# First eight projection tiles on raw activations, with the token's norm factor applied when they are copied out of PSUM

## What is computed

```
def rmsnorm(x, g):
    y = x * rsqrt(mean(x * x, axis=-1, keepdims=True) + EPS)
    return y * g

mk, mv = split(rmsnorm(mem, norm_mem) @ w_mem_kv)      # 256 memory rows
h = rmsnorm(x, norm_mix)
mq, mk, mv, mo, mi, mf, fq, fk, fv, ff, cq, gates = split_cols(h @ w_in)
qk_c, conv_new = causal_conv(conv_prev, concat([mq, mk]), conv_w, conv_b)
...                       # mLSTM, forgetting attention, cross-attention, gates, w_out
x = x + peer_ffn(rmsnorm(x, norm_ffn), ...)            # 16384 single-neuron experts
```

## Time and profile before

| | us |
|---|---|
| median of 3 runs | 2104.72 |
| lowest, highest | 2104.01, 2104.93 |
| the profiled execution | 2106.87 |
| its span in the trace | 2105.1 |
| PE busy (95% of the span) | 2004.1 |
| DVE busy (68%) | 1441.5 |
| ACT busy (39%) | 827.5 |
| POOL busy (38%) | 803.8 |

### The profile page before, as it was taken

The page is one execution under the profiler, slowest core; times in us unless marked ns, Lnnn a source line. Parts: engine busy times, 40 slices in busy tenths (PEclk is TensorE's granted clock), DMA queues, the critical chain, the costliest instruction groups (busy, mean ns, idle before and its releaser), DMA issues.

```text
span 2105.1 us, 34329 instructions
## 1 busy us (share of the span) xinstructions
PE 2004.1 (95%) x12622; PEld 1225.8 (58%) x12632; DVE 1441.5 (68%) x2699; ACT 827.5 (39%) x1223; POOL 803.8 (38%) x502
## 2 busy tenths in 40 slices
PE   5998998999999799999999999999899999999996
PEld 3745666667777577555555555555455555555553
DVE  5663554433335567889979999983687777777774
ACT  5334333434443322333445656663333333333331
POOL 5442111112233222466576666666343222222210
PEclk9999989999999899999999999999999999999998
DMA  5532112122344212357598999999999888889961
GB/s 200 133 129 93 41 50 79 69 73 79 139 135 132 92 61 73 134 184 243 206 336 306 351 356 359 353 358 390 354 377 369 335 331 330 330 333 342 338 236 45
DMA packets 180320, 467.11 MB, mean 222 GB/s; under 512 B 18600, under 2 KB 85168, under 8 KB 179448
## 3 DMA queue, kind: packets, MB, share of 16 engines
q1 hardware_dynamic: 102160, 248.28, 33.2%
q0 software_dynamic: 36864, 134.23, 17.4%
q10 hardware_dynamic: 41192, 83.22, 10.6%
HBM read 393.54 MB, written 72.14 MB: 221 GB/s over the span
## 4 chain that ended last, share of the span: by engine, by line
PE 81%; DVE 12%; DMA 3%; ACT 2%; issue 1%; POOL 1%; ACTq 0%; DVEq 0%
PE ps L1476 30%; PE ps L1836 27%; PE ps L1546 10%; PE ps L1492 3%; DMA rows<-in_u_rows,rowi 2%; PE ps L1693 2%; DVE rows L1322 1%; PE ps L1789 1%; PE ps L1790 1%; PE ps L1855 1%; PE ps L1658 1%; PE ps L1673 1%; PE ps L1752 1%; DVE eq L1309 1%; DMA raw<-in_v_units 1%
## 5 line engine op out<-in xcount | busy, mean ns | idle before, releaser
L479 POOL TENSOR_TENSOR w_lo<-raw,w_hi 128x1024 bf16<-128x1024 f32 x229 | 509.9, 2228 | 792.3 <-ACT w_hi L550 791.5
L550 ACT ACTIVATE w_hi<-raw 128x1024 bf16<-128x1024 f32 x357 | 375.2, 1052 | 505.3 <-PE ps L1836 299.2
L1476 PE MATMUL ps<-act_hi,w_hi 128*128 128x448 bf16 (+1 forms) x1424 | 445.6, 336 | 17.6 <-DVE act_lo L937 16.7
L1476 PE MATMUL ps<-act_lo,w_hi 128*128 128x448 bf16 (+1 forms) x1424 | 445.1, 336 | 0.0
L1476 PE MATMUL ps<-act_hi,w_lo 128*128 128x448 bf16 (+1 forms) x1424 | 445.0, 336 | 0.0
L1836 PE MATMUL ps<-W_hi,w_hi 128*128 128x448 bf16 x992 | 350.5, 353 | 7.0 <-DVE W_lo L1424 7.0
L1836 PE MATMUL ps<-W_hi,w_lo 128*128 128x448 bf16 x992 | 350.3, 353 | 0.0
L1836 PE MATMUL ps<-W_lo,w_hi 128*128 128x448 bf16 x992 | 350.3, 353 | 0.0
L492 POOL DMA_INDIRECT rows<-in_v_units,rowi x128 | 154.4, 1206 | 411.4 <-DVE accS L1419 394.9
L1405 DVE TENSOR_TENSOR w_lo<-raw,w_hi 128x1024 bf16<-128x1024 f32 x128 | 156.5, 1223 | 116.4 <-ACT w_hi L550 116.3
L1476 PEld LDWEIGHTS ps<-act_hi,w_hi 128*128 128x128 bf16 x1424 | 137.9, 98 | 123.0 <-issue 19.9
(11 more groups left out here) (333 smaller groups left out, 2937.5 us busy)
## 6 DMA issues: line engine op xcount, KB each, us to landing
raw<-in_u_units SPq DMA_DIRECT2D x128, 512.0 KB, 4.4
raw<-in_v_units SPq DMA_DIRECT2D x128, 512.0 KB, 9.3
raw<-in_units SPq DMA_DIRECT2D x101, 512.0 KB, 3.2
hd<-hb ACTq DMA_DIRECT2D x128, 224.0 KB, 5.2
gd<-gsb ACTq DMA_DIRECT2D x64, 448.0 KB, 6.4
Gb<-gd SPq DMA_DIRECT2D x32, 896.0 KB, 6.4
Hb<-hd SPq DMA_DIRECT2D x32, 896.0 KB, 8.2
gz<-stage ACTq DMA_DIRECT2D x24, 288.0 KB, 2.1
```

The source lines that it names most:

```text
L479: pool.tensor_tensor(w_lo[:, k % RING, :], raw[:, k % RAW, :], w_hi[:, k % RING, :], ALU.subtract).then_inc(lo_ready, 1)
L550: act.activation(w_hi[:, k % RING, :], raw[:, k % RAW, :], ACT.Copy).then_inc(hi_ready, 1)
L1476: last = pe.matmul(ps[:, bank + half, 0:n], w[:, slot, col:col + P], x(k)[:, half * n:(half + 1) * n], start=(k == 0 and w is w_hi and x i ...
```

## The change

- PE's eight tiles take `raw_hi` and `raw_lo`, the halves of `x * g` without the token's factor. ACT makes `raw_hi` by a copy with a scale, DVE `raw_lo` by one operation on `xT`, `par` and `raw_hi`.
- The factor is multiplied in where DVE copies a tile out: `copy_tile` is now a product of PSUM and `wk[:, 1, :]`. The tiles use three pairs of banks in turn (0 to 5), and tile k waits for the copy of tile k - 3.
- The factor is made for the token on the partition: five matmuls of one column (`spots`) sum the squares, ACT takes the root and DVE the reciprocal of 128 x 5 numbers (`rx`), and five matmuls with the identity spread them over banks 6 and 7, from where ACT copies 128 x 576 to `wk[:, 1, :]`. On PE the first five stand behind tile 0, the second five behind tile 1.
- `act_hi` and `act_lo`, with the factor, are still made, for what comes behind the eight tiles; DVE does so after it has copied out tiles 0 and 1, with tile 2's copy in the middle.
- `par` and weight unit 0 are loaded at once from SP, the table of the root is loaded while ACT waits for `xT`, and ACT casts units 0 to 3 between the eight blocks.
- PE's sums for the memory rows stand ahead of tile 6, in bank 6; ahead of tile 4 before.

```diff
@@ SP, ACT @@
+            sp.dma_start(par[:, :], a["par"]).then_inc(par_in, 16)
+            load(a["units"][0], 0, True, 0)
             sp.wait_ge(x_in[0], 16)
-            for n in range(RAW):
+            for n in range(1, RAW):
                 load(a["units"][n], n, True, 0)
...
-            act.dma_start(par[:, :], a["par"]).then_inc(par_in, 16)
...
             act.wait_ge(consts, 8)
-            square(xT, mix_sq, lambda k: (x_in[k // (KT // 2)], 16))
+            act.activation(warm[:, 3:4], epsb[:, 0:1], ACT.Sqrt)
             act.wait_ge(par_in, 16)
-            for n in range(RAW):
-                high_unit(n)
+            for k in range(KT):
+                act.wait_ge(x_in[k // (KT // 2)], 16)
+                act.activation(raw_hi[:, k, :], xT[:, k, :], ACT.Copy, scale=par[:, C_MIX + k:C_MIX + k + 1]).then_inc(x_hi, 1)
+                if k in (0, 3, 5, 7):
+                    high_unit((0, 3, 5, 7).index(k))
+                square(xT, mix_sq, None, [k])
...
-            root(0, wk[:, 1, :].rearrange("p (a b) -> p a b", a=2), ps[:, 0:2, 0:HALF])
+            root(0, rx[:, 0, :], ps[:, 6, 0:NTT])
+            act.wait_ge(r0_spread, 1)
+            act.activation(wk[:, 1, :], ps[:, 6:8, :].rearrange("p a b -> p (a b)")[:, 0:T], ACT.Copy).then_inc(r0_kept, 1)
             high(0, mix_h, act_hi)
...
@@ DVE @@
-            for k in range(1, KT):
-                add_square(0, k, mix_sq)
             dve.wait_ge(par_in, 16)
-            norm(0, xT, C_MIX, wk[:, 1, :], mix_h, act_hi, act_lo)
+            for k in range(KT):
+                dve.wait_ge(x_hi, k + 1)
+                dve.scalar_tensor_tensor(out=raw_lo[:, k, :], in0=xT[:, k, :], scalar=par[:, C_MIX + k:C_MIX + k + 1],
+                                         in1=raw_hi[:, k, :], op0=ALU.mult, op1=ALU.subtract).then_inc(x_lo, 1)
+                if k:
+                    add_square(0, k, mix_sq)
+            dve.wait_ge(n_rms, 1)
+            dve.reciprocal(rx[:, 1, :], rx[:, 0, :]).then_inc(n_inv, 1)
+            dve.wait_ge(r0_kept, 1)
...
                 dve.wait_ge(unit_used, U_T + k + 1)
-                dve.tensor_copy(proj[:, k, :].rearrange("p (a b) -> p a b", a=2),
-                                ps[:, 2 * (k % 2):2 * (k % 2) + 2, 0:HALF]).then_inc(t_evac, 1)
-
-            for k in range(3):
-                copy_tile(k)
+                dve.tensor_tensor(proj[:, k, :].rearrange("p (a b) -> p a b", a=2),
+                                  ps[:, 2 * (k % 3):2 * (k % 3) + 2, 0:HALF],
+                                  wk[:, 1, :].rearrange("p (a b) -> p a b", a=2), ALU.mult).then_inc(t_evac, 1)
+
+            copy_tile(0)
+            copy_tile(1)
+            scaled(0, xT, C_MIX, wk[:, 1, :], mix_h, act_hi, act_lo, lambda k: copy_tile(2) if k == 4 else None)
+            copy_tile(3)
             for k in range(1, KT):
                 add_square(1, k, mem_sq)
-            copy_tile(3)
+            copy_tile(4)
             norm(1, mem_x, C_MEM, wk[:, 0, 0:NMEM], mem_h, mem_hi, mem_lo)
-            for k in range(4, N_T):
+            for k in range(5, N_T):
                 copy_tile(k)
...
@@ PE @@
             pe.wait_ge(consts, 8)
-            sums(0, mix_sq, [ps[:, 0, 0:HALF], ps[:, 1, 0:HALF]], HALF)
-
-
-            pe.wait_ge(n_rms, 1)
...
             for k in range(N_T):
-                if k == 4:
-                    sums(1, mem_sq, [ps[:, 4, 0:NMEM]], NMEM)
+                if k == 6:
+                    pe.wait_ge(r0_kept, 1)
+                    sums(1, mem_sq, [ps[:, 6, 0:NMEM]], NMEM)
                 pe.wait_ge(lo_ready, U_T + k + 1)
-                if k >= 2:
-                    pe.wait_ge(t_evac, k - 1)
-                tile((U_T + k) % RING, a_hi, a_lo, 2 * (k % 2), ready=None if k else 0).then_inc(unit_used, 1)
-
+                if k >= 3:
+                    pe.wait_ge(t_evac, k - 2)
+                tile((U_T + k) % RING, *xg0, 2 * (k % 3), ready=None if k else 0, split=x_lo).then_inc(unit_used, 1)
+                if k == 0:
+                    pe.wait_ge(n_add, KT - 1)
+                    for t, t0 in enumerate(spots):
+                        last = pe.matmul(ps[:, 6, t:t + 1], mix_sq[:, 0, t0:t0 + P], ones[:, 0:1], start=True, stop=True)
+                    last.then_inc(n_ssq, 1)
+                if k == 1:
+                    pe.wait_ge(n_inv, 1)
+                    for t in range(4):
+                        pe.matmul(row0[:, t * P:(t + 1) * P], rx[:, 1, t:t + 1].broadcast_to((P, P)), ident[:, :], start=True,
+                                  stop=True)
...
```

More of the change, by code:

```diff
@@ L233, in program @@
         warm = sb("warm", [P, 4], F32)
+        rx = sb("rx", [P, 2, NTT], F32)
         ARENA = used[0]
@@ L252, in program @@
         mem_lo = place("mem_lo", V0 + 4096, [P, KT, NMEM], BF16)
+        raw_hi = place("raw_hi", V0 + 8192, [P, KT, T], BF16)
+        raw_lo = place("raw_lo", V0 + 8192 + KT * T * 2, [P, KT, T], BF16)
         mkT = sb("mkT", [P, HC, NMEM], F32)
@@ L391, in program @@
         comb_done, sp_ready = sem("comb_done"), sem("sp_ready")
+        x_hi, x_lo, r0_spread, r0_kept = sem("x_hi"), sem("x_lo"), sem("r0_spread"), sem("r0_kept")
         y_out = sem("y_out")
@@ L570, in _ @@
                 high_unit(n)
-            root(1, wk[:, 0, 0:NMEM], ps[:, 4, 0:NMEM])
+            root(1, wk[:, 0, 0:NMEM], ps[:, 6, 0:NMEM])
             high(1, mem_h, mem_hi)
@@ L930, in norm, with scaled @@
                 dve.wait_ge(n_inv, i + 1)
+                scaled(i, x, col, rs, h, hi, lo)
+            def scaled(i, x, col, rs, h, hi, lo, beside=lambda k: None):
                 for k in range(KT + 1):
+                    beside(k)
                     if k < KT:
@@ L1499, in _ @@
             pe.wait_ge(consts, 8)
-            sums(0, mix_sq, [ps[:, 0, 0:HALF], ps[:, 1, 0:HALF]], HALF)
-            pe.wait_ge(n_rms, 1)
+            spots = [t * P for t in range(4)] + [T - P]
+            row0 = ps[:, 6:8, :].rearrange("p a b -> p (a b)")
+            xg0 = (lambda k: raw_hi[:, k, :]), (lambda k: raw_lo[:, k, :])
             for k in range(N_T):
-                if k == 4:
-                    sums(1, mem_sq, [ps[:, 4, 0:NMEM]], NMEM)
+                if k == 6:
+                    pe.wait_ge(r0_kept, 1)
+                    sums(1, mem_sq, [ps[:, 6, 0:NMEM]], NMEM)
                 pe.wait_ge(lo_ready, U_T + k + 1)
-                if k >= 2:
-                    pe.wait_ge(t_evac, k - 1)
-                tile((U_T + k) % RING, a_hi, a_lo, 2 * (k % 2), ready=None if k else 0).then_inc(unit_used, 1)
+                if k >= 3:
[11 more added lines that the diff above has]
+                                  stop=True)
+                    pe.matmul(row0[:, TP:T], rx[TS:P, 1, 4:5].broadcast_to((P - TS, P)), ident[TS:P, TS:P], start=True,
+                              stop=True).then_inc(r0_spread, 1)
+            pe.wait_ge(n_lo, KT)
             pe.wait_ge(lo_ready, U_SMALL + 1)
```

## The result

| | median, us | lowest to highest | runs |
|---|---|---|---|
| before | 2104.72 | 2103.06 to 2106.75 | 11 |
| after | 2114.08 | 2109.27 to 2120.23 | 11 |

The ratio after to before is 1.0047, with a 95% interval of 1.0037 to 1.0057. The change makes the kernel 9.4 us slower, outside the range of the prediction and on the side to which it had given 0.07. The profiled execution has a span of 2113.4 us, against 2105.1.

A forecast was written before the change was run, and what follows sets the result against it. PE ends last in 81% of the span, so only its earlier start or shorter waits help. Tile 7's end -2.4, `mvN` +1.2 and clock +0.5 sum to -0.7, from median 2104.72 to 2104.0; range 2098.5 to 2107.

The forecast's parts named there:

- `mvN`: Behind the memory values: PE asks for bank 4 before ACT's late copy is done and waits 1.2 us, bounds 0 and 3.
- wrong if: Signs against the forecast: last addition done before 24, tile 1 taking 8 us or more, tile 4 not waiting for `w_lo`.
- x and unit 0: Start: x's first half, loaded beside unit 0 and `par`, lands at 7.5 instead of 6.44, bounds 6.4 and 7.8.
- DVE against POOL: Tile 0: DVE's low halves and additions alternate with POOL's low halves; holds cost 6.0 us, last addition at 27.6.
- the port costs little: Rival for tile 0: DVE's low halves slip between POOL's operations, last addition at 21.6, total 2096.8; chance 0.15.
- PE and its clock: Tiles 0 and 1 on PE: one-column products cost 1.2, tile 1 ends at 34.7; 0.5 counted for a low clock.
- the clock: Rival: fed in drips, PE runs at 1.2 GHz through tile 1, +5.9 of which 0.5 is counted, total 2109.4; chance 0.07.
- To unit 4: From the factor's spread at 36.0: unit 4 ready at 55.4, PE idle since 47.8, tile 4 at 55.5 instead of 58.6.
- Behind it: Behind tile 7: small loads later, units 12 to 15 cast at 83 to 87, SiLU 1 some 6.5 later, at 108.

The follow-up runs named there:

- g2: Changed kernel with ACT's cast of weight unit 0 moved from behind x block 0 to behind block 2; 2107.24 us in a single execution.
- h2: Changed kernel with packed convolution-state stores and ACT's cast of unit 0 behind x block 2 instead of block 0; 2103.08 us, ratio to before 0.9989.
- f1: Changed kernel with POOL's low halves of units 0 to 3 made over 16 of 1024 columns, the rest zero; 2102.46 us in a single execution.
- f4: Changed kernel with the convolution's state packed by ACT, so each store is 128 packets of 96 bytes instead of 1024 of 12; 2107.29 us, ratio 1.0007.
- e3: Changed kernel without the two stores of the convolution's state and the wait for them (two outputs missing); 2105.39 us, ratio to before 1.0006.
- f3: Kernel before with the convolution's state packed by ACT, each store 128 packets of 96 bytes instead of 1024 of 12; 2105.32 us, ratio 0.9998.
- f2: Kernel before with the casts of units 12 to 15 moved behind the convolution's two stores; 2114.29 us, ratio to before 1.0040.
- g1: Changed kernel, packed stores; casts of units 4 to 7 and memory's squares behind factor's root, units 12 and 13 before second root, small loads later; 2100.19 us, ratio 0.9984.
- g4: Changed kernel with POOL's low halves of units 0 to 3 over 16 columns only and packed convolution-state stores; 2099.34 us, ratio to before 0.9970.
- e2: Changed kernel with the nine small loads issued behind the memory values' store instead of behind the second norm; 2107.57 us, ratio to before 1.0019.
- g3: Changed kernel with packed convolution-state stores and the casts of units 4 to 7 and the memory's squares behind the factor's root; 2099.59 us, ratio 0.9973.
- h1: g3 with ACT's cast of unit 0 moved behind x block 2 as well; 2097.84 us, ratio to before 0.9966.

## Why the prediction was wrong

Forecast 2104.0, measured 2114.08. On the trace, the mark is 9.7 us late where the sum said 0.7 early, which is 10.4 us. Of these 8.2 are the stall at the memory keys, which had no term, and 3.7 stand ahead of tile 7's end (4.2 late, 0.5 of them counted); 1.2 for `mvN` did not come, and 0.3 go the other way. None of the three signs named as "wrong if" was seen (the last addition was out at 28.9, tile 1 took 7.3, tile 4 waited for `w_lo`): all three lie ahead of the step that cost most.

*x and unit 0: the term was put on the wrong load.* "I take 7.5, since the two start together", for x. x landed at 6.7, within the bounds; unit 0 at 10.2, where I had its cast done by 9.2. Bounds had been given for x's first half only, and the second half, which moves beside unit 0, was not in them. Moving ACT's order (g2, h2) is worth 2.2 us at the last addition.

*DVE against POOL: right.* The holds are there, one operation of DVE for each of POOL's four operations, and come to 6.5 us for 6.0. f1, without them, ends tile 0's additions 4.8 us sooner, at 24.1 and not at the 21.6 that I had without holds, since ACT's 2.7 us of waiting for unit 0 are still ahead of them. The rival "the port costs little" is out. By the Trainium skill (SBUF — State Buffer, SBUF: two separate sides) this lock is to be expected; the trace agrees, 2.68 for 0.75.

*PE and its clock: mis-sized.* I counted 0.5 for the clock. Measured: tile 0's last block 0.8 more, the one-column products 2.1 for 1.2, tile 1 7.3 (31.7 to 39.0) for 5.9, together 3.1. The rival "the clock" had the mechanism and its place, with a price of 5.9; the clock rose at 34.5, inside tile 1, and half of that came. What I held against it, that blocks 5 to 7 come 1.4 apart, did not hold: blocks 4, 5 and 6 came 3.3 apart, since POOL's operations ran some 2 us later than forecast, behind unit 0's landing, and the last two held additions there (20.07 and 23.41).

*To unit 4: right.* From the factor's spread to tile 4 19.4 us forecast, 19.1 measured; PE's idle time 7.7 forecast, 7.26 measured, released by `w_lo`. So tile 4 came 4.0 late by what stands ahead of the spread alone, and tile 7 ended at 86.5, 1.8 after before's instead of 2.4 ahead. Tiles 4 to 7 took what was forecast (27.0, forecast 26.8).

*Behind it: the step that failed.* "ACT gets to its nine small loads later and casts units 12 to 15 all at once at 83 to 87." I followed what this does to DVE (POOL's low halves) and not what it does to SP: the loads of units 16 to 19 wait for these low halves. The casts came at 86.8 to 90.7, 4 us late like all behind tile 1, and where the stall is absent the rest of the step is right too (SiLU 1 comes 24.1 us behind the small tile's start in f4, forecast 24.8). What failed is the queue that hangs on it: unit 16's load, issued at 90.5 behind the stores of 12-byte packets, took 14.8 us, and the prediction gave it nothing. The price is 8.2 us of PE; in the ratios to before it is 0.40% or 8.4 us (1.0047 to 1.0007). e3, f3 and f4 show the stores as what slows the load, f2 shows that the order of the casts alone does it in the old kernel as well.

*`mvN`: 1.2 forecast.* In the changed kernel nothing waits there, since the stall ahead gave ACT time. Where the stall is gone it is between 0 (e3, f4, g1, g4) and 1.9 (h2), with 0.7 to 1.0 in e2, g3 and h1.

On the medians: without the stall 1.0007; with unit 0's order 0.9989; with units 4 to 7 moved 0.9966. The first two are what the prediction had missed. Its own sum, -0.7 us, lies between 1.0007 and 0.9989.

What stays open: why packets of 4 KB stay slow for 12 us behind 12-byte stores of which most have left the queue's records by 92. The Trainium skill (DMA: Bandwidth & Descriptors, Specifications) gives 512 B as the smallest transfer for full rate, and a read-modify-write below it. By that the 96-byte packets should suffer too; here 256 of them landed in 3.0 and 3.9 us (f4) or 1.5 and 1.6 (f3), and the load behind them took 3.2 us in f3. No run here tells whether the count of packets or their size decides.

## What to carry to other kernels

When a step is moved later on an engine that feeds a ring of buffers, follow the ring backwards as well: who refills the buffer, when, and what other transfers stand there at that hour. A store of many short pieces is cheap until a load behind it is needed at once; pack it into one row for each partition first. And a freed engine is a place for work: the same four casts gained nothing ahead of the root, where VectorE and GpSimd were in each other's way, and behind it, where VectorE was idle, they and the memory's squares gained some 7 us.
